# A hybrid decoder trunk on one core: partial norm sums on TensorE, an earlier weight load, and two waits moved

## The reference, cut to what matters

```python
def rms_norm(x, g, eps=RMS_EPS):
    xf = x.astype(jnp.float32)
    y = xf * lax.rsqrt(jnp.mean(xf * xf, axis=-1, keepdims=True) + eps)
    return (y * g.astype(jnp.float32)).astype(x.dtype)

def hgrn2_mixer(h, S0, w_in, lb, g_norm, w_out):
    ...
    f = lb + (1.0 - lb) * jax.nn.sigmoid(fz)
    log_f = jnp.log(jnp.maximum(f, HG_F_MIN))
    k = (1.0 - lb) * jax.nn.sigmoid(-fz)
    q = jax.nn.silu(q.astype(f32))
    ...
    o = o.reshape(B, T, D_MODEL).astype(h.dtype) * jax.nn.sigmoid(g)
    return rms_norm(o, g_norm) @ w_out, S

for i in range(DEPTH):
    h = rms_norm(x, W['norm_mix'][i])
    ...
    x = x + mixed
    x = x + swiglu(rms_norm(x, W['norm_ffn'][i]), W['ffn_w_in'][i], W['ffn_w_out'][i])
y = rms_norm(x, W['final_norm'])
```

## Time and profile before

| | us |
|---|---|
| median of 3 runs | 3368.26 (3367.2 to 3368.73) |
| profiled execution | 3362.62 |
| its span, first to last instruction | 3361.0 |
| TensorE busy, by the page | 3209.1 (95%) |
| VectorE, ScalarE, GpSimd busy | 1832.5, 1080.8, 131.4 |
| mean granted TensorE clock | 0.985 |

### The profile page before, as it was taken

One profiled execution on the slowest core, in us unless ns is written; L12 is line 12 of the kernel. 1 busy time (PEld: TensorE's weight loads), 2 busy tenths in 40 slices (PEclk: granted clock), 3 DMA queues, 4 the chain that ended last, 5 costly groups with the idle time before them and its releaser, 6 DMA issues.

```text
span 3361.0 us, 82189 instructions
## 1 busy us (share of the span) xinstructions
PE 3209.1 (95%) x35272; PEld 3041.2 (90%) x35272; DVE 1832.5 (55%) x3017; ACT 1080.8 (32%) x1754; POOL 131.4 (4%) x247
## 2 busy tenths in 40 slices
PE   8998999999998999997999999899999999899998
PEld 7887899998787999996988888899999888799998
DVE  6666643445655543437367887543344666654343
ACT  3222321223555321222434443332223222332221
POOL 0000000001322000000000000000000000000000
PEclk9999999999999999998999999899999999999999
DMA  3322222223433332221210000222232222223222
GB/s 124 102 83 65 85 89 88 86 98 96 129 119 97 87 95 81 88 93 61 82 34 19 12 20 15 61 88 92 83 97 78 84 89 83 71 83 96 81 91 77
DMA packets 104598, 269.08 MB, mean 80 GB/s; under 512 B 12802, under 2 KB 45954, under 8 KB 104146
## 3 DMA queue, kind: packets, MB, share of 16 engines
q1 hardware_dynamic: 91346, 228.54, 21.8%
q0 software_dynamic: 13056, 37.64, 3.4%
HBM read 247.60 MB, written 18.52 MB: 79 GB/s over the span
## 4 chain that ended last, share of the span: by engine, by line
PE 82%; DVE 9%; ACT 3%; DVEq 3%; issue 2%; DMA 1%; SPq 1%; ACTq 0%; POOLq 0%; POOL 0%
PE ps L573 66%; PE ps L1016 5%; DVE arena_r L1924 1%; PE ps L1008 1%; PE ps L654 1%; PE ps L1112 1%; DVE cell L2241 1%; PE ps L712 1%; DVEq L2070 1%; PE ps L735 1%; DVE h L2238 1%; DMA ring<-in_w_mix 1%; DVE arena L2366 1%; DVEq L2240 0%; DVE arena_r L1930 0%
## 5 line engine op out<-in xcount | busy, mean ns | idle before, releaser
L573 PE MATMUL ps<-arena_r 128*128 128x272 f32 x11136 | 1500.7, 293 | 78.2 <-DVE arena_r L1917 22.8
L573 PEld LDWEIGHTS ps<-arena_r 128*128 128x128 f32 x11136 | 1429.9, 190 | 127.3 <-issue 64.1
L573 PE MATMUL ps<-hb_r,arena_r 128*128 128x272 f32 x8448 | 1059.5, 287 | 0.4 <-DVE hb_r L1917 0.4
L573 PEld LDWEIGHTS ps<-hb_r,arena_r 128*128 128x128 f32 x8448 | 1057.4, 188 | 1.1 <-DVE hb_r L1917 0.8
L1415 ACT ACTIVATE arena_r<-ring 128x1024 fp32r<-128x1024 f32 (+1 forms) x240 | 275.8, 1149 | 910.0 <-PE ps L573 910.0
L1943 DVE TENSOR_TENSOR arena_r<-ring,arena_r 128x1024 fp32r<-128x1024 f32 (+1 forms) x240 | 319.7, 1332 | 143.5 <-ACT arena_r L1415 143.5
L1991 DVE TENSOR_TENSOR arena<-ps,rstd 128x544 f32<-128x544 f32 x88 | 63.7, 724 | 291.6 <-PE ps L573 291.6
L2012 DVE TENSOR_TENSOR x<-x,ps 128x544 f32<-128x544 f32 x64 | 46.2, 722 | 291.8 <-PE ps L573 291.8
L1397 ACT ACTIVATE arena_r<-ring 128x1024 fp32r<-128x1024 f32 x80 | 84.8, 1060 | 137.6 <-PE ps L573 132.6
L1462 ACT ACTIVATE arena_r<-arena 128x544 f32 (+1 forms) x88 | 58.2, 661 | 196.0 <-DVE arena L1996 196.0
L1924 DVE TENSOR_TENSOR arena_r<-ring,arena_r 128x1024 fp32r<-128x1024 f32 x80 | 97.6, 1220 | 34.7 <-ACT arena_r L1397 21.9
(11 more groups left out here) (406 smaller groups left out, 3070.2 us busy)
## 6 DMA issues: line engine op xcount, KB each, us to landing
ring<-in_w_up SPq DMA_DIRECT2D x176, 512.0 KB, 3.5
ring<-in_w_mix SPq DMA_DIRECT2D x112, 512.0 KB, 3.5
ring<-in_w_down SPq DMA_DIRECT2D x64, 704.0 KB, 4.0
arena<-in_hg_s POOLq DMA_DIRECT2D x16, 512.0 KB, 3.8
out_hg_so<-arena POOLq DMA_DIRECT2D x16, 512.0 KB, 2.9
ring<-in_w_hgout SPq DMA_DIRECT2D x16, 512.0 KB, 3.5
arena<-in_cache_k SPq DMA_DIRECT2D x128, 64.0 KB, 1.9
arena<-in_cache_v POOLq DMA_DIRECT2D x128, 64.0 KB, 2.2
```

The lines of the kernel that those rows point to most:

```text
L573: mm = pe.matmul(PS[:, 2 * a + hf, 0:HALF], part[:, ws], rhs[:, o:o + HALF], start=start and n == 0, stop=stop and n == 2)
```

## The change

Five edits. (1) RWKV's input norm takes the folded form of the final norm, with the same functions (`folded`, `folded_root`, `folded_factor`, `normed_chunk`); the split of weight unit 1 goes from before the norm to behind its root and reciprocal, and unit 1 follows unit 0 by one block. (2) HGRN's output norm: TensorE multiplies the sum of seven heads and the last head's square separately (`norm_part`), the first before and the second between the last products of output blocks 0 and 1; VectorE's last addition goes away, and in the loop its addition stands before the eviction of unit 3. The last chunk's remainder is made before the state updates. TensorE waits for the root at block 2 instead of 3 and for the states at block 3 instead of before the norm; VectorE's wait for the states' store goes behind the output product. (3) In every HGRN head k and q are made before f, and the first level is released by q. (4) In the attention the first weight unit of head 1 is issued ahead of the cached keys of head 0 and not after them. (5) The attention's signs, with the wait for their constants, are computed after the first eviction of queries.

```diff
         def sums(name):
-            return sum(KC if n.endswith("o") else KC - 1 for n in norms[:nth(name)])
+            return sum(KC - 2 if plain(n) else KC - 1 for n in norms[:nth(name)])
...
                 sp.wait_ge(S("norm_rms"), nth(norm_name(layer, "m")) + 1)
+                load(1, 0, 4)
                 cached_keys(0)
-                with sp.Fori(1, HEADS - 1) as h:
-                    for n, row in enumerate((0, -1, 1)):
+                def second_head_on(h, n0):
+                    for n, row in list(enumerate((0, -1, 1)))[n0:]:
                         load(h, n, h * 4 + row)
                     no_load(h, 3)
                     sp.wait_ge(S("at_ss_mm"), h)
                     cached_keys(h)
+                second_head_on(1, 1)
+                with sp.Fori(2, HEADS - 1) as h:
+                    second_head_on(h, 0)
...
+            def norm_part(squares, a, first):
+                for hf in range(2):
+                    mm = pe.matmul(PS[:, 2 * a + hf, 0:HALF], const("ones"), squares[:, hf * HALF:(hf + 1) * HALF],
+                                   start=first, stop=not first, skip_group_check=True)
+                return mm
+            def folded(name):
+                for last in range(2):
+                    if last:
+                        pe.wait_ge(S("norm_sq"), KC * nth(name) + KC)
+                    else:
+                        pe.wait_ge(S("norm_acc"), sums(name) + KC - 2)
+                    src = nm_sq[(KC - 1) % 2] if last else nm_acc
+                    for q in range(4):
+                        mm = pe.matmul(PS[q * 32:(q + 1) * 32, 0, 0:NT // 4], const("ones")[:, 0:32],
+                                       src[:, q * (NT // 4):(q + 1) * (NT // 4)], start=not last, stop=bool(last), skip_group_check=True)
+                mm.then_inc(S("norm_ssq"), 1)
+                pe.wait_ge(S("fin_r"), nth_plain(name) + 1)
+                for q in range(4):
+                    rows = slice(q * 32, (q + 1) * 32)
+                    mm = pe.matmul(PS[:, 4 + q, 0:NT // 4], const("ones")[rows, :], rstd[rows, 0:NT // 4], start=True, stop=True)
+                mm.then_inc(S("fin_mm"), 1)
...
+                name_o = norm_name(layer, "o")
+                pe.wait_ge(S("norm_acc"), sums(name_o) + KC - 1)
+                pe.wait_ge(S(L + "out"), HEADS * (j + 1) + 1)
+                norm_part(nm_acc, 2, True)
                 out_block(0, KC - 1)
+                pe.wait_ge(S("norm_sq"), KC * nth(name_o) + KC)
+                norm_part(nm_sq[0], 2, False).then_inc(S("norm_ssq"), 1)
                 out_block(1, KC - 1)
-                pe.wait_ge(S(L + "state"), HEADS * (j + 1) + 1)
-                norm(norm_name(layer, "o"), 3)
                 for m in range(2, KC):
+                    if m == 2:
+                        pe.wait_ge(S("norm_rms"), nth(name_o) + 1)
                     if m == 3:
-                        pe.wait_ge(S("norm_rms"), nth(norm_name(layer, "o")) + 1)
+                        pe.wait_ge(S(L + "state"), HEADS * (j + 1) + 1)
...
             def rwkv(layer):
-                norm(norm_name(layer, "m"), 0)
+                folded(norm_name(layer, "m"))
...
                 for c in range(KC):
                     unit_block(0, c)
-                    unit_block(1, c)
+                    if c:
+                        unit_block(1, c - 1)
+                unit_block(1, KC - 1)
...
             def rwkv(layer):
-                root(norm_name(layer, "m"), 0)
+                folded_root(norm_name(layer, "m"))
+                rw_split(layer, 1)
...
+            def normed_chunk(gain, c):
+                h, x = (ap[:, c, :].rearrange("p (q t) -> p q t", q=4) for ap in (h3, x3))
+                dve.scalar_tensor_tensor(h, x, vec3[:, gain, c:c + 1], PS[:, 4:8, 0:NT // 4], ALU.mult, ALU.mult)\
+                   .then_inc(S("norm_h"), 1)
...
+                    dve.tensor_scalar(hg_ks[:, 0:NT], hg_sgn, scratch[:, 1:2], None, ALU.mult)
+                    dve.tensor_tensor(hg_q, hg_qs, hg_qr, ALU.mult).then_inc(S(L + "lvl"), 1)
                     dve.tensor_scalar(hg_f, hg_sgp, scratch[:, 1:2], scratch[:, 3:4], ALU.mult, ALU.add)
-                    dve.tensor_scalar(hg_ks[:, 0:NT], hg_sgn, scratch[:, 1:2], None, ALU.mult)
-                    dve.tensor_tensor(hg_q, hg_qs, hg_qr, ALU.mult)
                     dve.drain()
-                    dve.tensor_scalar(hg_f, hg_f, F_MIN, None, ALU.max).then_inc(S(L + "lvl"), 1)
+                    dve.tensor_scalar(hg_f, hg_f, F_MIN, None, ALU.max)
...
+                    if not more:
+                        low(L, 2 * KC * j + KC, V_HG + j, o3, hh, hl, KC - 1)
                     for b in range(NB):
                     ...
                     if more:
                         hg_rest(layer, h + 1, 4)
+                        dve.wait_ge(S("norm_sq"), h + (KC * nth(name_o) - j * HEADS + 1))
+                        dve.tensor_tensor(nm_acc, nm_acc, nm_sq[0], ALU.add).then_inc(S("norm_acc"), 1)
                         evict(h + 1, 3)
-                    else:
-                        low(L, 2 * KC * j + KC, V_HG + j, o3, hh, hl, KC - 1)
-                    dve.wait_ge(S("norm_sq"), h + (KC * nth(name_o) - j * HEADS + 1))
-                    dve.tensor_tensor(nm_acc, nm_acc, nm_sq[0], ALU.add).then_inc(S("norm_acc"), 1)
...
-                dve.wait_ge(S(L + "st_free"), HEADS * (j + 1) + 1)
                 for m in range(KC):
                 ...
+                dve.wait_ge(S(L + "st_free"), HEADS * (j + 1) + 1)
...
-                dve.wait_ge(S("at_c_in"), 16)
-                signs = at_const("signs")
-                dve.scalar_tensor_tensor(c_sign, signs[:, 1:2], c_nlam, signs[:, 0:1], ALU.mult, ALU.add)
                 factor(norm_name(layer, "m"))
...
                 query_evict(0)
+                dve.wait_ge(S("at_c_in"), 16)
+                signs = at_const("signs")
+                dve.scalar_tensor_tensor(c_sign, signs[:, 1:2], c_nlam, signs[:, 0:1], ALU.mult, ALU.add)
...
-                factor(norm_name(layer, "m"))
+                folded_factor(norm_name(layer, "m"))
+                rw_rest(layer, 1)
...
+                dve.wait_ge(S("fin_mm"), nth_plain(norm_name(layer, "m")) + 1)
                 normed_input(0)
```

More of the change, by code:

```diff
@@ L558, in norm @@
             def norm(name, a):
-                pe.wait_ge(S("norm_acc"), sums(name) + (KC if name.endswith("o") else KC - 1))
+                pe.wait_ge(S("norm_acc"), sums(name) + KC - 1)
                 for hf in range(2):
@@ L1350, in _ @@
                 feed_forward(layer)
-            for last in range(2):
-                if last:
-                    pe.wait_ge(S("norm_sq"), KC * nth("nfin") + KC)
-                else:
-                    pe.wait_ge(S("norm_acc"), sums("nfin") + KC - 2)
-                src = nm_sq[(KC - 1) % 2] if last else nm_acc
-                for q in range(4):
-                    mm = pe.matmul(PS[q * 32:(q + 1) * 32, 0, 0:NT // 4], const("ones")[:, 0:32], src[:, q * (NT // 4):(q + 1) * (NT // 4)],
-                                   start=not last, stop=bool(last), skip_group_check=True)
-            mm.then_inc(S("norm_ssq"), 1)
-            pe.wait_ge(S("fin_r"), 1)
-            for q in range(4):
-                rows = slice(q * 32, (q + 1) * 32)
-                mm = pe.matmul(PS[:, 4 + q, 0:NT // 4], const("ones")[rows, :], rstd[rows, 0:NT // 4], start=True, stop=True)
-            mm.then_inc(S("fin_mm"), 1)
+            folded("nfin")
         @block.scalar
@@ L1436, in after_feed_forward @@
                         at_split(layer + 1, 0, c - (KC - 2))
-                if layer + 1 == LAYER_RW and c >= KC - 2:
-                    rw_split(layer + 1, c - (KC - 2))
                 square(norm_name(layer + 1, "m") if layer + 1 < depth else "nfin", x3, c)
+                if layer + 1 == LAYER_RW and c == KC - 2:
+                    rw_split(layer + 1, 0)
             def feed_forward(layer):
@@ L1548, in hgrn @@
                     if m == 0:
-                        root(name_o, 3)
+                        root(name_o, 2)
                     after_mixer(layer, m)
@@ L1904, in factor, with folded_factor @@
                 dve.drain()
+            def folded_factor(name):
+                dve.wait_ge(S("norm_rms"), nth(name) + 1)
+                dve.reciprocal(rstd[:, 0:NT // 4], rstd[:, 0:NT // 4]).then_inc(S("fin_r"), 1)
+            def normed_chunk(gain, c):
+                h, x = (ap[:, c, :].rearrange("p (q t) -> p q t", q=4) for ap in (h3, x3))
+                dve.scalar_tensor_tensor(h, x, vec3[:, gain, c:c + 1], PS[:, 4:8, 0:NT // 4], ALU.mult, ALU.mult)\
+                   .then_inc(S("norm_h"), 1)
             def add_squares(name, c):
@@ L1959, in after_feed_forward @@
                         at_rest(layer + 1, 0, c - (KC - 2))
-                if layer + 1 == LAYER_RW and c >= KC - 2:
-                    rw_rest(layer + 1, c - (KC - 2))
-                if layer + 1 < depth:
```

(13 more changed lines are left out.)

21 lines of the change are left out of this document (10 added, 11 removed).

## The result

| | before | after |
|---|---|---|
| median of the runs beside each other | 3367.73 (3366.88 to 3368.73, 4 runs) | 3342.01 (3339.82 to 3346.11, 4 runs) |
| profiled execution; its span | 3362.62; 3361.0 | 3341.62; 3340.0 |
| TensorE busy; mean granted clock | 3209.1; 0.985 | 3203.8; 0.989 |

What follows compares the result with a forecast made beforehand. TensorE bounds the kernel, busy 3209.1 of 3361.0 us. Gains 5.2 + 8.4 + 4.6 + 0.9 = 19.1 took the profiled 3362.62 to 3343.5; the median's 5.6 offset gave 3349.2, range 3343 to 3358.

Steps and rivals of the forecast that it cites:

- RWKV's entry: RWKV's folded norm: first normed chunk 5.4 us after the last feed-forward sum starts instead of 10.6, gain 5.2 us.
- attention's entry: Attention's start: earlier reciprocal, earlier weight load for head 1 and full clock together gain 8.4 us.
- HGRN, output to first sum, both layers: End of both HGRN mixers: reciprocal starts sooner after the last head's output, 2.5 and 2.1 us, sum 4.6.
- last heads: Last head of each HGRN layer: first level starts 1.4 us sooner, mostly lost at later levels; 0.9 us in all.
- the order of the units: RWKV's entry: unit 1 one block behind leaves six more products after the last chunk; hidden, otherwise costs 0.9 us.
- its three terms (4.1, 2.0, 2.3): Attention's entry: reciprocal not waiting for constants 4.1 us, head 1's weights loaded sooner 2.0, full TensorE clock 2.3.
- Rival A: Gaps passed on: attention's clock still falls or load lands late, HGRN keeps one microsecond per layer; 3356.5 us, chance 0.15.
- the table load: HGRN ends: ScalarE's load takes 1.28 us without the skill's 1.38 drain, which would make the total gain 2.8 less.
- the gap of 2.36 before 354.97 stays, so the layer is worth 2.5: HGRN layer 0's end: block 3 still waits for a remainder hanging on the reciprocal, so the layer gains 2.5 us.
- Rival B: More than the sum: last heads keep full clock, up to 1.6 us each, RWKV's remainder hides; 3345 us, chance 0.12.
- Rival C: Slower: addition moved ahead of unit 3's eviction makes VectorE late at 14 HGRN heads' starts; 3375 us, chance 0.03.
- Rival D: Waits move but no end does: a further wait the trace doesn't show; 3363 to 3370 us, chance 0.07.

Runs made afterwards that it cites:

- the experiment: VectorE's wait for the state's store put back ahead of the output product, against the changed kernel: 3355.76 us, the changed kernel beside it 3346.44.

## Why the prediction came out low in its gain

The gain by place, from the stretches of all traces with and without each part:

| place | forecast | measured | bounds given |
|---|---|---|---|
| RWKV's entry | 5.2 | 4.9 | 4.3 to 5.6 |
| attention's entry | 8.4 | 7.5 | 4.1 to 8.9 |
| HGRN, output to first sum, both layers | 4.6 | 4.9 | 2.5 to 5.5 |
| HGRN, clock behind the gap before block 3 | 0 | 1.9 | none |
| last heads | 0.9 | 0.7 | 0 to 4 |
| sum | 19.1 | 19.9 | |

The row of the last heads is weak: a last head takes 34.8 to 36.5 us from one execution to the next, with and without the edits.

**RWKV** went as written; only the order of the units had been guarded by an end of its own (0.9) and cost nothing that could be seen. Two small slips in the working changed nothing: the copy ends at 3.14 + 1.06 = 4.2, not 4.1, and the upper bound should have been 10.6 - 5.15 = 5.4, not 5.6.

**Attention.** Idle time, twelve products and scores came within 0.1 us of their forecasts. The 8.4 was read against one trace whose entry took 33.8 us, the longest of six; against their mean it is 7.5. What the prediction did not see is that its three terms (4.1, 2.0, 2.3) cannot be had one by one. They were right as a sum only because both edits are in: the load is the condition for the other edit's 4.1, and both are the condition for the clock. Rival A's case, a clock that falls all the same, did not come in any of the six traces with both edits.

**HGRN.** That the store's wait costs nothing at its new place was right, and the experiment shows what the move was worth: 6 us a layer once the states are updated later. On the table load the row had decided against the added drain that the Trainium skill, "ScalarE: Activation LUTs", section "What ACT_TABLE_LOAD costs", gives. The trace of after agrees with the row: load at 342.84 for 1.28, root at 344.13, 0.01 behind it. So the 2.8 us by which the page would have lowered the sum did not appear.

The step that failed is "the gap of 2.36 before 354.97 stays, so the layer is worth 2.5". The gap stayed (2.54), the low clock behind it did not, so the term that the prediction put at nothing without a reason was worth 1.9 us on average over the traces, and 3.0 between the two profiled executions, in which neither layer has the low stretch any more (first to last sum into x 39.3 us before, 37.8 after). Windows of TensorE around block 3, layers 0 and 3, before:

```profile
354.00:364.00 10.00, 9.03 (x60) 0.83 0.16 52
2918.00:2928.00 10.00, 10.00 (x68) 0.83 0.16 51
```

after:

```profile
353.00:363.00 10.00, 9.29 (x74) 1.00 0.27 92
2896.00:2906.00 10.00, 9.08 (x72) 1.00 0.27 94
```

and in the trace of the five rounds of the changed kernel:

```profile
353.00:363.00 10.00, 10.00 (x70) 0.84 0.15 46
2896.00:2906.00 10.00, 9.31 (x74) 1.00 0.30 94
```

From the first sum into x to the fifth it is 21.2 to 21.3 us in every layer of every trace without HGRN's part; with it and this gap (four traces: the changed kernel three times and HGRN's part alone), 19.95 in layer 3 of all four and in layer 0 of one, and 21.27 in layer 0 of the other three. That is 1.3 + 0.3 = 1.6, and 0.3 more for the last blocks of the product, which go along. I had bounded every term but this one: the gap stayed, and I took its low clock as staying with it. What else had changed lies ahead of the gap. Before, the last products of blocks 0 and 1 already ran at a low clock (0.67 from 340.5 to 343 us, 0.56 from there to 345); after, the same windows have 1.00. That alone does not decide: the trace of the five rounds has 1.00 there too (338 to 345 us), and its block 3 in layer 0 was low all the same. Of the eight layers of these four traces the three with a low block 3 are those whose last head had also taken longer (36.1 to 36.3 us, against 34.9 to 35.5 in the five clean ones). Without the part block 3 was low behind short and long last heads alike, and the gap before it was 2.3 us in nine layers and 3.1 to 3.3 in seven. So the same gap in the same code is followed by a low stretch in one execution and not in another. Whether the last head's clock bears on block 3's, or both follow from something else, was not tried, and the cause stays open. Taking the gap away settles it in practice, as far as one trace can show: with block 3's weights made earlier both layers are clean, behind a last head of 36.1 us too.

**The last heads** gave 0.7, not to be told from nothing, with the clock low all the same: its mean is 0.51 from 314 to 319 us in the trace of after (0.66 before). Rival B's time, 3345, is the nearest to what was measured, but its mechanism, the full clock in the last heads, did not come; the surplus that the traces show came from block 3. Rival A's sum keeps 2.5 of HGRN where its words say one microsecond per layer, which makes no difference here.

**The sum.** All executions taken together, 35 of the kernel before (mean 3365.8) and 13 of the changed one (mean 3344.6), put the change at 21.2 us, with a standard error of 1.3. The forecast of 19.1 lies within two standard errors, and the table explains 19.9. Of the 7.2 us between 3349.2 and the first result, 2.1 are gain not forecast (the clock behind block 3's gap, above all), 2.5 come from the baseline, the median of three runs at 3368.3 where the mean of 35 is 3365.8, and 2.6 from the four runs after, which lay below the mean of 13. Those last two are chance as far as the record shows, and with the means in their place the time would have been 3344.6, inside the range. So the mechanism was right, one term was missing, and the range, whose lower end allowed 2 us for the measurement, was too narrow for a kernel of which single executions lie 10 us apart (before) and 15 (after).

Rival C has nothing for it: VectorE's reordered addition made no head late: from the first head's output to the seventh's it is 222.1 us in layer 0 and 222.4 in layer 3, before and after. Rival D is out with the stretches above.

## What to carry to other kernels

Two waits one behind the other in the same entry can be worth little each (1.2 and 0.3 us here) and all of their sum together (7.5): before pricing one, move it in thought and read who is late next, then price the pair. When work is moved ahead of a store, the wait for that store moves with it, and the store may come to lie behind a weight load, where it took 5.4 us here instead of 2.9. Behind a gap that stays, the clock may still change; so the low stretch is a term of its own, with ends of its own, and a baseline of three runs is no better known than its spread.

## What the runs showed of the hardware that was not expected

The number of low-clock stretches differs between executions of the same program, away from any gap worth the name: RWKV's heads took 296.4 us at a clock of 1.00 and 305.7 at 0.97 on identical instructions, the largest single difference seen in this case, and larger than any one edit. No idle time of TensorE in these heads is longer than 0.6 us in any trace, and from 1761 to 1768 us in the second execution of the changed kernel it is busy for 7.00 of 7.00 us at a mean clock of 0.76.

Product loops in the feed-forward differ as well, at the full clock: the first half of layer 0's takes 195.85 us in the first trace of the kernel before and 197.41 in the first of the changed one, with a mean clock of 1.00 and 1566 records in both. From the seventh attention head to the middle of the next feed-forward layer, which no edit touches, it is 208.9 to 212.4 us over the traces. What selects the one or the other was not found.

A store of 512 KB landed 2.9 us after its issue when it went ahead of a weight load of the same size and 5.3 to 5.8 us when it went behind it.

Of TensorE's gaps, those of 1.4 and 1.5 us were not followed by a low stretch (the attention's entry in six traces, before output block 2 in the ten layers of five traces); those of 5.4 us and more at the attention's entry always were (the load alone and the kernels without this part); the gap before block 3 was in all sixteen layers of the traces without HGRN's part, where it is 2.3 to 3.3 us long, and in three of eight with it, where it is 2.5.
